# Attention and out-projection of a decoder trunk: exponentials released by the maximum alone, a z_u chunk split around the turns, and a new order in the out-projection's first unit

## What is computed

```python
h = x @ w_in                       # u (512) | v (512) | q (512) | k (128) | v (128)
z_u = gelu(h[..., :512]); z_v = layer_norm(gelu(h[..., 512:1024]))
A = z_u * chunk_spatial(z_v)       # gate, by blocks of 128 positions
q, k = rotary(q), rotary(k)        # 8 query heads, 2 kv heads of 64
s = q . k / 8, banded: window 128, in blocks of 128 queries x 256 keys
m = max(max(s), sink);  p = exp(s - m);  p /= sum(p) + exp(sink - m)
B = p . v
x = layer_norm(alpha * x + concat(A, B) @ w_out)
x = layer_norm(alpha * x + conv_ffn(x))
```

## Time and profile before

| | |
|---|---|
| time, median of 3 executions | 2292.27 us (2290.54 to 2292.74) |
| the profiled execution: its time, its span in the trace | 2287.8 us, 2286.1 us |
| TensorE busy | 2183.1 us, 95% of the span |
| VectorE busy | 1653.5 us, 72% |
| ScalarE busy | 980.4 us, 43% |
| GpSimd busy | 825.8 us, 36% |
| chain that ended last, by engine | PE 79%, DVE 14%, ACT 4%, issue 2%, POOL 1% |

### The profile page before, as it was taken

One profiled execution on the slowest core, in us unless ns is written; L12 is line 12 of the kernel. 1 busy time (PEld: TensorE's weight loads), 2 busy tenths in 40 slices (PEclk: granted clock), 3 DMA queues, 4 the chain that ended last, 5 costly groups with the idle time before them and its releaser, 6 DMA issues.

```text
span 2286.1 us, 35544 instructions
## 1 busy us (share of the span) xinstructions
PE 2183.1 (95%) x14132; PEld 1985.6 (87%) x14132; DVE 1653.5 (72%) x2018; ACT 980.4 (43%) x1773; POOL 825.8 (36%) x444
## 2 busy tenths in 40 slices
PE   7999999799999999999999999979999999999996
PEld 7997677799999998888799877769999999988885
DVE  1477767777788876787636687677778778767676
ACT  3226755444434434343322276454434443443332
POOL 1115255454455450320311242545455545311311
PEclk9999999899999999999999999999999999999998
DMA  5313166122332326666552122641232233375762
GB/s 158 86 36 78 40 189 192 47 67 77 88 86 60 86 73 217 224 217 208 168 140 48 50 49 93 177 147 52 81 86 73 72 88 86 96 253 184 240 217 92
DMA packets 208765, 269.74 MB, mean 118 GB/s; under 512 B 31952, under 2 KB 167376, under 8 KB 208528
## 3 DMA queue, kind: packets, MB, share of 16 engines
q1 hardware_dynamic: 208600, 267.46, 39.0%
HBM read 217.65 MB, written 46.13 MB: 115 GB/s over the span
## 4 chain that ended last, share of the span: by engine, by line
PE 79%; DVE 14%; ACT 4%; issue 2%; POOL 1%; DMA 0%; SPq 0%; ACTq 0%; DVEq 0%; POOLq 0%
PE ps L2080 40%; PE ps L1799 18%; PE ps L1764 9%; PE ps L2019 5%; DVE bnst L1260 1%; PE ps L1824 1%; DVE rl L1439 1%; PE ps L1903 1%; DVE rzc L1246 1%; PE ps L1929 1%; PE ps L1882 1%; DVE cb L1512 1%; PE ps L1918 1%; DVE Sb L1558 1%; PE ps L1828 1%
## 5 line engine op out<-in xcount | busy, mean ns | idle before, releaser
L2080 PE MATMUL ps<-bt,bh 128*128 128x272 f32 x3520 | 588.5, 290 | 19.4 <-issue 15.5
L2080 PEld LDWEIGHTS ps<-bt,bh 128*128 128x128 f32 x3520 | 502.2, 190 | 20.3 <-issue 20.3
L946 ACT ACTIVATE bh<-wblk 128x512 fp32r<-128x512 f32 x308 | 183.4, 623 | 487.9 <-POOL wblk L753 249.3
L2080 PE MATMUL ps<-bt,bl 128*128 128x272 f32 x1760 | 366.4, 290 | 0.0
L2080 PEld LDWEIGHTS ps<-bt,bl 128*128 128x128 f32 x1760 | 277.1, 190 | 0.0
L741 POOL TENSOR_TENSOR bl<-wblk,bh 128x512 fp32r<-128x512 f32 x98 | 164.6, 1683 | 297.5 <-ACT bh L946 297.5
L1799 PE MATMUL ps<-rh,ah 128*128 128x512 f32 x792 | 245.5, 391 | 5.8 <-DVE ah L1450 5.2
L1799 PE MATMUL ps<-rl,ah 128*128 128x512 f32 x792 | 244.1, 389 | 0.0
L2080 PE MATMUL ps<-ba,bh 128*128 128x272 f32 x1408 | 233.7, 288 | 1.7 <-POOL bl L741 1.7
L1439 DVE TENSOR_TENSOR rl<-wrow,rh 128x1024 fp32r<-128x1024 f32 x132 | 191.3, 1451 | 42.7 <-ACT rh L1002 42.2
L1363 DVE TENSOR_TENSOR bl<-wblk,bh 128x512 fp32r<-128x512 f32 x210 | 171.8, 851 | 62.2 <-ACT bh L946 62.2
(11 more groups left out here) (216 smaller groups left out, 4029.2 us busy)
## 6 DMA issues: line engine op xcount, KB each, us to landing
wrow<-in_w_down SPq DMA_DIRECT2D x132, 512.0 KB, 4.7
wblk<-in_w_up SPq DMA_DIRECT2D x88, 512.0 KB, 5.3
a_scr<-hg SPq DMA_DIRECT2D x44, 552.0 KB, 3.5
araw<-a_scr SPq DMA_DIRECT2D x88, 192.0 KB, 4.2
wrow<-in_w_out SPq DMA_DIRECT2D x48, 256.0 KB, 5.1
wrow<-in_w_out SPq DMA_DIRECT2D x24, 512.0 KB, 4.2
wraw<-in_w_in SPq DMA_DIRECT2D x10, 1024.0 KB, 6.0
z_scr<-rzc SPq DMA_DIRECT2D x16, 512.0 KB, 5.0
```

The source lines that it names most:

```text
L946: act.activation(bh[b][:], block_of(f, b), ACT.Copy).then_inc(S["u_hi"], 1)
L2080: e = nc.tensor.matmul(out[:, n, :], lhs, rhs[:, HW_ // 2 * n:HW_ // 2 * n + HW_ // 2], start=(k == 0 and m == 0), stop=(k == HK - 1 and m ...
```

## The change

It has four parts. **Exponentials:** ScalarE's exponentials wait for `a_m` where they waited for `a_neg`; the sink's small exponential still waits for `a_neg`. **Split chunk:** the last chunk of each block is cut at `ZK = 5` of its 8 slices of k. TensorE now does the first five slices, `scores(b+1, 0)`, `turned(b, 0)`, the last three slices, `turned(b, 1)`, the V transpose, `scores(b+1, 1)` and `values(b)`. ScalarE's copy of that chunk, with the weight row's rounding where there is one, moves behind the copies to `pTb`. **VectorE's order:** `softmax_out(b, 0)` goes ahead of the `vring` copy, and `gate(0)` behind block 3's `softmax_out(3, 1)`. **Out-projection's first unit** (`g = kk = 0`): it waits for the high left tiles, does the three tiles' high x high and high x low, waits for `m_lo(l, 0)`, and does low x high last; what follows the unit is as before.

```diff
 # ScalarE
-                        act.wait_ge(S["a_neg"], 2 * n + hf + 1)
+                        act.wait_ge(S["a_m"], 2 * n + hf + 1)
                         for h in range(4 * hf, 4 * hf + 4):
                             act.activation(Sb[:, h, :], Sb[:, h, :], ACT.Exp, bias=ast[:, 1, h:h + 1],
                                            accum_out=ast[:, 3, h:h + 1])
+                        act.wait_ge(S["a_neg"], 2 * n + hf + 1)
                         act.activation(ast[:, 4, 4 * hf:4 * hf + 4], ...)
-                    for u in range(ZAT[b], ZAT[b + 1]):
+                    for u in range(ZAT[b], ZAT[b + 1] - 1):
                         zu_evac(u)
...
                             act.activation(dst, src, ACT.Copy).then_inc(S["a_ptev"], 1)
+                    zu_evac(ZAT[b + 1] - 1)
                     if b == 2:
                         zu_gelu(0)
 # VectorE
                     softmax_in(b, 1)
+                    softmax_out(b, 0)
                     dve.wait_ge(S["pe_vtr"], n + 1)
                     after(dve, "pe_pv", n)
                     dve.tensor_copy(vring[:, b % 2, :], ps[:, 7, 0:P]).then_inc(S["a_vr"], 1)
+                    softmax_out(b, 1)
                     if b == 3:
                         gate(0)
-                    softmax_out(b, 0)
-                    softmax_out(b, 1)
 # TensorE: chunk(slot, c, bank, k0=0, k1=KD) and zu(u, k0=0, k1=KD) now take a range of k
-                    for u in range(ZAT[b], ZAT[b + 1]):
+                    for u in range(ZAT[b], ZAT[b + 1] - 1):
                         zu(u)
+                    u = ZAT[b + 1] - 1
+                    zu(u, 0, ZK)
+                    if b < NB - 1:
+                        scores(b + 1, 0)
+                    turned(b, 0)
+                    zu(u, ZK, KD)
+                    turned(b, 1)
                     if b < NB - 1:
                         values_in(b + 1)
-                        scores(b + 1, 0)
-                    turned(b, 0)
-                    turned(b, 1)
-                    if b < NB - 1:
                         scores(b + 1, 1)
                     values(b)
...
                         right = out_hi(KD * g + kk)
+                        if g == 0 and kk == 0:
+                            pe.wait_ge(S["m_hi"], len(M_OPS) * l + 1)
+                            for i in range(3):
+                                out_part(g, i, kk, 0, right, start=True)
+                            low = out_lo(0)
+                            for i in range(3):
+                                e = out_part(g, i, kk, 0, low)
+                            e.then_inc(S["c_used"], 1)
+                            pe.wait_ge(S["m_lo"], len(M_OPS) * l + 1)
+                            for i in range(3):
+                                e = out_part(g, i, kk, 1, right)
+                            e.then_inc(S["c_hused"], 1)
+                            samp[kk]()
+                            continue
```

More of the change, by code:

```diff
@@ L45 @@
 ZC = [2, 1, 1, 2, 1, 1, 1, 1]
+ZK = 5
 ZAT = [2 + sum(ZC[:b]) for b in range(NB + 1)]
@@ L1805, in body, with chunk @@
             def body(l):
-                def chunk(slot, c, bank):
+                def chunk(slot, c, bank, k0=0, k1=KD):
                     a, b = CH[c]
-                    pass3(ps[:, bank, 0:b - a], [((wh[slot % 2][:, k, :], wl[slot % 2][:, k, :]), (xh[:, k, a:b], xl[:, k, a:b]))
-                                                 for k in range(KD)]).then_inc(S["in_done"], 1)
+                    out, n = ps[:, bank, 0:b - a], slot % 2
+                    for k in range(k0, k1):
+                        for m, (lhs, rhs) in enumerate(((wh, xh), (wh, xl), (wl, xh))):
+                            e = nc.tensor.matmul(out, lhs[n][:, k, :], rhs[:, k, a:b], start=(k == 0 and m == 0), stop=(k == KD - 1 and m == 2))
+                    if k1 == KD:
+                        e.then_inc(S["in_done"], 1)
                 def two_chunks(c):
@@ L1884, in body, with zu @@
                     e.then_inc(S["g_pe"], 1)
-                def zu(u):
-                    if u % 3 == 0:
+                def zu(u, k0=0, k1=KD):
+                    if u % 3 == 0 and k0 == 0:
                         pe.wait_ge(S["w_lo"], l * WIO + 10 + u // 3 + 1)
@@ L1890, in zu @@
                         pe.wait_ge(S["in_ev"], l * NZ + 9)
-                    else:
+                    elif k0 == 0:
                         pe.wait_ge(S["zu_ev"], l * 12 + u - 1)
-                    chunk(u // 3, u % 3, u % 2)
+                    chunk(u // 3, u % 3, u % 2, k0, k1)
                 def scores(b, hf):
@@ L2030, in body @@
                                 pe.wait_ge(S["ln_r"], ln_n(l, 0, C3[g - 1][i]) + 1)
-                            if g == 0 and i == 0 and kk in (0, HK):
-                                pe.wait_ge(S["m_lo"], len(M_OPS) * l + 1 + kk // HK)
+                            if g == 0 and i == 0 and kk == HK:
+                                pe.wait_ge(S["m_lo"], len(M_OPS) * l + 2)
                             elif g == 1 and kk == 0:
```

## The result

The changed kernel takes 2294.39 us (median of 12 runs, 2291.98 to 2298.74) where the kernel before takes 2289.93 us (12 runs, 2286.95 to 2294.59): a ratio of 1.0024, 95% interval 1.0016 to 1.0032. That ratio is 5.5 us of 2290; the two medians alone differ by 4.5. Forecast were 6.5 us more, 2298.8 us, on a median that was then 2292.27; 2294.39 lies in the range of 2288 to 2303.

What follows compares the result with a forecast made beforehand. TensorE was taken as busy nearly throughout, VectorE with under 1 us to spare in block 2. Per layer 2.65 + 0.6 = 3.25 us, 6.5 in two layers, gave 2298.8 us; range 2288 to 2303.

Steps and rivals of the forecast that it cites:

- -4.9 + 0.8 + 0.4 + 0.7 + 0.6: Per layer: waits taken away, chunk entries, last block's wait, its values' wait, and ScalarE's later output copy.
- 1.75 + 1.4 + 2.5: TensorE's new waits per layer: 1.75 us in blocks 1, 2, 4; 1.4 in block 5; 2.5 behind the gate.
- The split chunk, taken away: Between the two turns of each block: the chunk's rest covers the copy waits, up to 4.2 us per layer.
- The entry of a chunk: TensorE enters a chunk once more per block: 0.10 us each, 0.8 us per layer.
- The gate: First z_u pair's gate, now ahead of block 4's first mask, delays its second scores: 2.5 us, bounds 0 and 2.6.
- it does what it says: Rival: the chunk's rest covers the copy and VectorE's room suffices; -2.4 us per layer, 2287.5 us; chance 0.17.
- GpSimd's hold: Rotations hold VectorE's steps, so first turns wait: 0.15 us in block 1, 0.8 in 2 and 4, 1.4 in 5.
- The exponentials' wait: Exponentials may start 0.2 to 1.2 us earlier, shortening a half's chain but gaining no VectorE time.
- Block 7 and the end: Last block: no scores between chunk and turn, so 0.4 us of waiting; its values still wait 0.7 for the copies.
- ScalarE's late copy: End of the values: ScalarE copies the attention output 0.6 us later per layer.
- the stop ahead of the samples: TensorE's wait for the samples' probabilities grows from 2.06 to some 3.2 us.
- The clock behind the samples' stop: Lower TensorE clock after that stop: layer 0 pays already; 0.8 us for layer 1 only in the upper bound.

Runs made afterwards that it cites:

- e6_late_rotation: e1_gate_back with GpSimd's rotation for a block begun only after block b-2's second multiplication, not with that block's second scores: 2279.92 us, ratio 0.9951.
- e3_no_rotation: The changed kernel with GpSimd's three rotation instructions cut to 4 of 128 queries from block 2 on: 2283.83 us, ratio 0.9968.
- e1_gate_back: The changed kernel with gate(0) back ahead of block 3's softmax_out(3, 0): 2286.27 us, ratio 0.9983.
- e8_gate_back_neg: e1_gate_back with the exponentials waiting for a_neg (the difference to the sink) again: 2290.18 us, ratio 0.9998.
- e7_max_only: The kernel before with the exponentials' wait alone changed: 2286.36 us, ratio 0.9991.
- e4_unit_only: The kernel before with the out-projection's first unit in the new order alone: 2291.37 us, ratio 1.0002.
- e9_late_rotation_zk6: e6_late_rotation with the chunk cut at 6 of 8 slices: 2284.24 us, ratio 0.9975.
- e2_gate_moved: The kernel before with gate(0) behind block 3's second softmax_out and nothing else: 2292.75 us, ratio 1.0018.
- e11: The kernel before with only GpSimd's rotation made to wait for block b-2's second multiplication: 2292.84 us, ratio 1.0013.

## Why the forecast came out as it did

The direction and the mechanism were right. That the sum came near was luck: two groups of its terms were too small, on opposite sides. The undisturbed rows of the new order (layer 0 of e6_late_rotation, with layer 1's 10.41 for block 1, where there is no wait) sum to 120.57 us, 5.3 below the kernel before; e3_no_rotation has the same rows to 0.01 us but for the gate's. The same terms of the forecast, -4.9 + 0.8 + 0.4 + 0.7 + 0.6, make -2.4. On top come the waits with the clock behind them: 7.5 us in layer 0 and 8.2 in layer 1 (without the event of its start), where 1.75 + 1.4 + 2.5 = 5.65 were forecast. So 3.25 us per layer met 2.16 and 2.88.

- **The split chunk, taken away: mis-sized.** The forecast took the 4.2 us that the profile names as waits. By starts, a turn's eight transposes take 0.85 us, and the second turn came 1.44 to 2.21 us after the first, eight of them together 12.85: 6.05 us of standing time. The V transpose gained too: from the second turn to the second scores took 1.07 us (261.31 to 262.38) with the V transpose's 0.20 at another place, and takes 1.07 now with it in between (263.91 to 264.98). Half of that goes again at the place it left: the first scores start 0.27 after the chunk's last matmul (260.07 to 260.34), the V transpose started 0.18 after it. The entry of a chunk cost 0.10 as assumed, 262.25 to 262.52 against 0.175. A quiet 384-column block went from 11.05 to 10.41 (layer 1, block 0 to 1), 0.64 where the working gave 0.30.
- **The gate: right place, price too low.** 2.5 us forecast; 0.72 and 2.36 us of waits, then 1.6 to 3.0 us at the lower clock. The forecast had put the clock only behind the samples' stop. e1_gate_back shows that the move is the whole loss: the rival "it does what it says" had 2.4 us of gain per layer, and 1.5 and 1.4 came without the move, with GpSimd's holds still in it.
- **GpSimd's hold: right mechanism, sizes and one block off.** e3_no_rotation removes the waits. Forecast were 0.15, 0.8 and 0.8 us in blocks 1, 2 and 4 and 1.4 in block 5; layer 0 had 0.54, 0.28, none and 1.11, and layer 1 none, 0.27, none and 1.11. Block 4's is absent behind the gate's stop; with the gate back (e1_gate_back) it is there, 0.45. In block 5 the row's subtraction and the rotations follow each other as described, and the small steps took 0.70 and 1.22. The Trainium skill, page "SBUF — State Buffer", section "Who interferes with whom", says that the issue order decides which of the two blocks; the trace agrees: in that block GpSimd's third instruction, which started at 249.69 when VectorE's multiplication of 248.72 was under way, took 2.13 us instead of 1.29.
- **The exponentials' wait: "gains no VectorE time", costed at nothing, is worth 0.77 and 0.55 us per layer** in the new order by e8_gate_back_neg, 0.16 in the old by e7_max_only.
- **Block 7 and the end.** 0.4 forecast, 0.25 measured; the values' 0.7 stayed; ScalarE's late copy 0.6 forecast, 0.5 measured; the stop ahead of the samples 3.2 forecast, 2.83. That the out-projection's first unit brings nothing is shown by e4_unit_only.
- **The clock behind the samples' stop.** Forecast: layer 0 pays as before, layer 1 may pay 0.8 us. In the trace layer 1 did pay and layer 0 no longer: 17.6 us from the turn on have a mean of 1.00 in layer 0 (0.90 before) and 0.91 in layer 1 (1.00 before). The price was far below 0.8 us: from the samples' turn to the first turn of a normalised tile it took 17.41 and 17.26 us before, 17.27 and 17.34 after, so 0.1 us.

## What to carry to other kernels

When work is put into a gap, count the gap by starts, not by the idle time that the profile names, and then look at the engine that feeds both ends of it: here the gain of 1.5 us per layer was real, and one 2.4 us instruction at a new place in VectorE's queue cost more than it. GpSimd's work beside VectorE's small two-input steps is worth moving as a whole: one changed wait, together with the gate's old place, gave the 0.49% that none of the parts gave alone. A gain that rests on a gap of a tenth of a microsecond (e6_late_rotation against e9_late_rotation_zk6) has to be measured again after each edit.

## What the runs showed of the hardware

Short stops have an uncertain second price. The stop behind the gate, 0.72 and 2.36 us with 1.2 us of work between (e3_no_rotation: 1.96 alone), was followed by a granted clock of 0.50 to 0.63 in all four layers seen; e2_gate_moved's shorter stops at that place, 0.71 and 1.18 us, stayed at 1.00. Block 7's two waits in the old order, 1.18 and 0.74 us, were followed by it in four of ten layers (kernels before, e2, e4, e7, e11), 1.5 us each time; in the new order, with 0.16 to 0.26 and 0.74 us, in none of eighteen. So the split also took away a cost that the trace of the kernel before happened not to show. The Trainium skill, page "TensorE: Matmul & The Clock Gate", section "Part 1: The HAM clock gate", says of the slow matmuls at a kernel's start that their number varies from run to run of the same kernel. These ten layers agree in kind, in mid-kernel: the same waits to 0.01 us, and either clock.
